# A two-layer decoder trunk: key products on GpSimd, a third weight tile, y turned tile by tile, state copies in sixteen parts

## The reference

```python
def trunk_layer(x, start_pos, conv_buf, pool_buf, k_buf, v_buf, ...):
    h = rms_norm(x, norm_g)
    proj = jnp.einsum('btd,de->bte', h, w_in)
    a_val, a_glu, a_gate, b_val, b_gate, q, k, v, c_gate = jnp.split(proj, cuts, axis=-1)
    u = a_val * jax.nn.sigmoid(a_glu)
    u_ext = jnp.concatenate([conv_buf, u], axis=1)
    c = layer_norm(causal_dwconv(u_ext, conv_w, conv_b), ln_g, ln_b)
    ya = jax.nn.silu(c) * jax.nn.silu(a_gate)
    new_conv = u_ext[:, -(CONV_W - 1):]
    pb_ext = jnp.concatenate([pool_buf, b_val], axis=1)
    yb = multiscale_pool(pb_ext, start_pos, pool_w, pool_scale) * jax.nn.silu(b_gate)
    new_pool = pb_ext[:, -POOL_BUF:]
    q = rope(rms_norm(q, qn_g), pos); k = rope(rms_norm(k, kn_g), pos)
    kk = jnp.concatenate([k_buf, k], axis=1); vv = jnp.concatenate([v_buf, v], axis=1)
    o = dilated_attention(q, kk, vv, k_buf.shape[1])     # 3 patterns: (128,1),(512,4),(2048,16)
    yc = o.reshape(B, T, C_ATT) * jax.nn.silu(c_gate)
    y = jnp.einsum('bte,ed->btd', jnp.concatenate([ya, yb, yc], axis=-1), w_out)
    return x + y, new_conv, new_pool, kk[:, -n_keep:], vv[:, -n_keep:]
```

## Time and profile before

| | us |
|---|---|
| three runs | 416.89, 414.5, 413.16 |
| median | 414.5 |
| the profiled execution, its time | 414.18 |
| its span, first to last instruction | 412.4 |

### The profile page before, as it was taken

One profiled execution on the slowest core, in us unless ns is written; L12 is line 12 of the kernel. 1 busy time (PEld: TensorE's weight loads), 2 busy tenths in 40 slices (PEclk: granted clock), 3 DMA queues, 4 the chain that ended last, 5 costly groups with the idle time before them and its releaser, 6 DMA issues.

```text
span 412.4 us, 4549 instructions
## 1 busy us (share of the span) xinstructions
PE 353.1 (86%) x1552; PEld 272.6 (66%) x1552; DVE 232.0 (56%) x522; ACT 103.3 (25%) x243; POOL 46.3 (11%) x87
## 2 busy tenths in 40 slices
PE   1489799994779969989998999998488968989993
PEld 1368688883457755558876888887366754558872
DVE  1334769859984786331113589979986786331010
ACT  3120013532152422310112011533143422311013
POOL 2410011111101101110010001111111011210000
PEclk9999989999797997999999999999969999999998
DMA  8999999999999999999999999999999999999984
GB/s 282 415 419 417 419 414 360 393 408 378 407 405 417 413 389 385 387 351 418 419 401 412 412 408 381 398 415 351 376 403 418 414 374 370 383 348 333 325 326 186
DMA packets 48836, 158.06 MB, mean 383 GB/s; under 512 B 4644, under 2 KB 18670, under 8 KB 47998
## 3 DMA queue, kind: packets, MB, share of 16 engines
q0 software_dynamic: 21824, 95.11, 60.4%
q1 hardware_dynamic: 17812, 39.36, 25.3%
q10 hardware_dynamic: 9178, 23.31, 14.5%
HBM read 149.39 MB, written 104.42 MB: 615 GB/s over the span
## 4 chain that ended last, share of the span: by engine, by line
PE 46%; DVE 18%; SPq 16%; DMA 14%; issue 2%; ACT 2%; ACTq 0%; DVEq 0%
PE pj L571 17%; PE pj L710 14%; SPq L378 10%; DMA kv<-in_cache_v_win 7%; PE psc L642 7%; DMA kv<-in_cache_k_win 6%; SPq L436 5%; DVE kv L1088 4%; DVE ssc L1091 4%; DVE yc L1148 3%; PE ptr L497 2%; PE ps L519 2%; DVE sc L1058 1%; PE ps L687 1%; PE ps L693 1%
## 5 line engine op out<-in xcount | busy, mean ns | idle before, releaser
L571 PE MATMUL pj<-hT,w 128*128 128x264 f32 x800 | 193.6, 401 | 8.6 <-DVE hT L1010 5.8
L571 PEld LDWEIGHTS pj<-hT,w 128*128 128x128 f32 x800 | 156.1, 198 | 40.2 <-issue 10.3
L1148 DVE SCALAR_TENSOR_TENSOR yc<-u_ext,par,yc 128x256 f32<-128x256 f32 x180 | 76.2, 481 | 2.8 <-DVE u_smp L1038 0.6
L710 PE MATMUL pj<-mix,w 128*128 128x264 f32 x256 | 59.3, 386 | 0.0
L710 PEld LDWEIGHTS pj<-mix,w 128*128 128x128 f32 x256 | 48.5, 190 | 8.2
L485 POOL DMA_DIRECT2D out<-in_cache_v_win x48 | 25.8, 542 | 172.1 <-issue 172.1
L1218 DVE TENSOR_TENSOR xT<-xT,pj 128x264 f32<-128x264 f32 x16 | 6.9, 429 | 53.6 <-PE pj L710 53.6
L485 POOL DMA_DIRECT2D out<-in_cache_k_win x32 | 18.7, 587 | 138.5 <-issue 130.7
L831 ACT ACTIVATE ex<-pj 128x264 f32<-128x264 f32 x22 | 8.6, 391 | 82.6 <-PE pj L571 66.1
L642 PE MATMUL psc<-kv,spm 128*48 128x384 f32 x80 | 27.8, 500 | 1.4 <-DMA kv<-in_cache_v_win 1.4
L937 ACT ACTIVATE hT<-xT 128x264 f32<-128x264 f32 x16 | 6.8, 423 | 66.1 <-DVE xT L1218 66.1
(11 more groups left out here) (169 smaller groups left out, 330.3 us busy)
## 6 DMA issues: line engine op xcount, KB each, us to landing
out<-in_cache_k_win POOLq DMA_DIRECT2D x32, 1512.0 KB, 71.8
out<-in_cache_v_win POOLq DMA_DIRECT2D x16, 1152.0 KB, 72.0
out<-in_cache_v_win POOLq DMA_DIRECT2D x17, 1080.0 KB, 71.1
w<-in_w_out ACTq DMA_DIRECT2D x2, 4096.0 KB, 28.7
out<-in_cache_v_win POOLq DMA_DIRECT2D x16, 432.0 KB, 72.2
w<-in_w_in ACTq DMA_DIRECT2D x1, 4608.0 KB, 31.0
kv<-in_cache_k_win SPq DMA_DIRECT2D x32, 144.0 KB, 24.5
w<-in_w_in ACTq DMA_DIRECT2D x3, 1536.0 KB, 27.6
```

Of the source, the lines that this page charges most:

```text
L571: last = nc.tensor.matmul(pj[n % RING][:, 0:T], wbuf[buf][:, k, col:col + P], hT[:, k, :], start=(k == 0), stop=(k == KD - 1))
L710: last = nc.tensor.matmul(pj[n % RING][:, 0:T], w1[:, k, m * P:(m + 1) * P], mix[:, k, :], start=(k == 0), stop=(k == KD - 1))
L1148: last = V.scalar_tensor_tensor(out=yc[:, t, 0:SEQ], in0=x_w, scalar=par[:, ROW_CW + w * CT + t:ROW_CW + w * CT + t + 1], in1=yc[:, t, 0:S ...
```

## The change

- VectorE's ten products move to GpSimd (`product`), in its queue ahead of copies 20 to 24 (layer 0) and 54 to 58 (layer 1). The first of a layer waits for the gathered keys and for `qb`. VectorE's `sscore` keeps the sums; the five steps stand one projection later in the list, the fifth behind `vtok` 1.
- A third tile `w2` takes b_val and b_gate. So `w0` columns 0 to 767 are free after layer 0's a_glu, and layer 1's a_val and a_glu are loaded behind layer 0's value gather, a_gate once c_gate (now in a_gate's columns) is used.
- In the last layer each tile of `xT` is turned by PE as soon as it is added (`turn_y`), in place of its sum of squares and ACT's Square; ACT, and for one of the four pieces VectorE, copies halves of 4 tiles, and SyncE stores y in five parts.
- The state copies are cut into 16 by 8 pieces in place of 8 rows.
- `so` (output of the sample attention) shares the memory of `rep`, and `spT` turns 48 rows in place of 128; its memset goes.

The diff, cut to what the text speaks of:

```diff
@@ -81,9 +81,9 @@
 PROJ += [("q", t, "w1", t * P) for t in range(AT)]
 PROJ += [("k", t, "w1", C_ATT + t * P) for t in range(AT)]
 PROJ += [("v", t, "w1", 2 * C_ATT + t * P) for t in range(AT)]
-PROJ += [("c_gate", t, "w0", 2 * C_POOL + t * P) for t in range(AT)]
-PROJ += [("b_val", t, "w0", t * P) for t in range(PT_)]
-PROJ += [("b_gate", t, "w0", C_POOL + t * P) for t in range(PT_)]
+PROJ += [("c_gate", t, "w0", 2 * C_CONV + t * P) for t in range(AT)]
+PROJ += [("b_val", t, "w2", t * P) for t in range(PT_)]
+PROJ += [("b_gate", t, "w2", C_POOL + t * P) for t in range(PT_)]
 NPROJ = len(PROJ)
 PIDX = {(g, t): n for n, (g, t, _, _) in enumerate(PROJ)}
 GATES = [(g, t) for g, t, _, _ in PROJ if g in ("a_glu", "a_gate", "c_gate", "b_gate")]
@@ -103,11 +103,11 @@
 SV_CUTS = [(0, 8), (8, 16), (16, SLOTS + 1)]
 _behind = {
     5: ["st0"], 6: ["st1"], 8: ["sconv"],
-    10: [("norm", 0), "conv_p"], 11: [("norm", 1), "conv_s"], 12: [("norm", 2), "rep_q"], 13: [("norm", 3), "qb", ("sscore", 0)],
-    14: [("norm", 4), ("sscore", 1)], 15: [("norm", 5), ("sscore", 2)],
-    16: [("score", 0), "rep_k", ("sscore", 3), ("pnorm", 0)],
-    17: [("probT", 0), ("score", 1), "kb", ("sscore", 4), ("pnorm", 1), "rep_v"],
-    18: [("probT", 1), ("score", 2), ("vtok", 0), ("vtok", 1), ("pnorm", 2), "snew", ("out", 0)],
+    10: [("norm", 0), "conv_p"], 11: [("norm", 1), "conv_s"], 12: [("norm", 2), "rep_q"], 13: [("norm", 3), "qb"],
+    14: [("norm", 4), ("sscore", 0)], 15: [("norm", 5), ("sscore", 1)],
+    16: [("score", 0), "rep_k", ("sscore", 2), ("pnorm", 0)],
+    17: [("probT", 0), ("score", 1), "kb", ("sscore", 3), ("pnorm", 1), "rep_v"],
+    18: [("probT", 1), ("score", 2), ("vtok", 0), ("vtok", 1), ("sscore", 4), ("pnorm", 2), "snew", ("out", 0)],
     19: [("probT", 2), ("score", 3), ("out", 1), "vb", ("pnorm", 3), "ssoft0"],
     20: [("probT", 3), ("score", 4), ("out", 2), ("ktok", 0), ("pnorm", 4), "ssoft1"],
     21: [("probT", 4), ("score", 5), ("out", 3), ("ktok", 1), ("pnorm", 5)],
@@ -176,6 +176,7 @@
 COPIES = [("k", s, a, a + HALF_ROWS) for s in range(NS) for a in (0, HALF_ROWS)]
 COPIES += [("v", s, a, b) for s in range(NS) for a, b in ((0, 768), (768, EVEN_ROWS), (FAR_LO, GATHER[0][0]))]
 IN_FLIGHT = 16
+PRODUCT_AHEAD_OF = {20 + i: (0, i) for i in range(len(SCORE_CUTS))} | {54 + i: (1, i) for i in range(len(SCORE_CUTS))}
 assert DEPTH * len(COPIES) % IN_FLIGHT == 0
 XROUNDS = 5
 
...
@@ -422,10 +425,7 @@
             sp.dma_start(cst[:, early:], const[:, early:]).then_inc(const_in, 16)
 
             for l in range(DEPTH):
-                if l > 0:
-                    sp.wait_ge(S["pj_full"], nth(l - 1, "pj_full", NPROJ))
-                    weights(l, w0, 0, "w_in", COL["a_val"], 3 * C_CONV, "a_in")
-                else:
+                if l == 0:
                     weights(l, w0, 2 * C_CONV, "w_in", COL["a_gate"], C_CONV, "a_gate_in")
 
                 sp.wait_ge(zeroed, 1)
@@ -442,39 +442,62 @@
                     for name in ("v_near_out", "v_far_out"):
                         sp.wait_ge(S[name], nth(l - 1, name, per[name]))
                 gather("k", l, "k_in")
-                sp.wait_ge(S["pj_full"], nth(l, "pj_full", PIDX[("a_gate", CT - 1)] + 1))
-                weights(l, w0, 0, "w_in", COL["b_val"], 2 * C_POOL, "b_in")
+                if l > 0:
+                    sp.wait_ge(S["pj_full"], nth(l - 1, "pj_full", NPROJ))
+                weights(l, w2, 0, "w_in", COL["b_val"], 2 * C_POOL, "b_in")
                 gather("v", l, "v_in", "ks_used")
+                if l < DEPTH - 1:
+                    sp.wait_ge(S["pj_full"], nth(l, "pj_full", PIDX[("a_glu", CT - 1)] + 1))
+                    weights(l + 1, w0, 0, "w_in", COL["a_val"], 2 * C_CONV, "a_val_in")
                 for name, out, keep in (("state_conv", o_conv_s, TAIL - 1), ("state_pool", o_pool_s, POOL_BUF - 1)):
-                    sp.dma_start(out[bass.ds(l, 1), :, 0:keep].rearrange("o s w c -> (o s) (w c)"),
-                                 one(name, l)[:, :, 1:keep + 1].rearrange("o s w c -> (o s) (w c)"))\
+                    sp.dma_start(out[bass.ds(l, 1), :, 0:keep].rearrange("o s w c -> (o s) (w c)").rearrange("s (e x) -> e s x", e=16),
+                                 one(name, l)[:, :, 1:keep + 1].rearrange("o s w c -> (o s) (w c)").rearrange("s (e x) -> e s x", e=16))\
                         .then_inc(S["state_out"], 16)
                 if l < DEPTH - 1:
+                    sp.wait_ge(S["pj_full"], nth(l, "pj_full", PIDX[("c_gate", AT - 1)] + 1))
+                    weights(l + 1, w0, 2 * C_CONV, "w_in", COL["a_gate"], C_CONV, "a_gate_in")
                     params(l + 1)
                     states(l + 1)
                 sp.wait_ge(S["v_in"], nth(l, "v_in", per["v_in"]))
                 put_back_values(l)
-            for r in range(2):
-                sp.wait_ge(y_copied, 2 * r + 2)
-                sp.dma_start(y_prompt.rearrange("b (r p) d -> r p (b d)", p=P)[r], x_tok[:, r * D_MODEL:(r + 1) * D_MODEL]).then_inc(y_out, 16)
-            sp.wait_ge(y_copied, XROUNDS)
+            y_rows = y_prompt.rearrange("b (r p) d -> r p (b d)", p=P)
+            sp.wait_ge(y_copied, 1)
+            sp.dma_start(y_rows[0][:, 0:512], x_tok[:, 0:512]).then_inc(y_out, 16)
+            sp.wait_ge(y_copied, 2)
+            sp.dma_start(y_rows[1][:, 0:512], x_tok[:, D_MODEL:D_MODEL + 512]).then_inc(y_out, 16)
+            sp.wait_ge(y_copied, 4)
+            sp.dma_start(y_rows[0][:, 512:], x_tok[:, 512:D_MODEL]).then_inc(y_out, 16)
+            sp.wait_ge(y_half_copied, 1)
+            sp.dma_start(y_rows[1][:, 512:], x_tok[:, D_MODEL + 512:2 * D_MODEL]).then_inc(y_out, 16)
+            sp.wait_ge(y_copied, 5)
             sp.dma_start(y_sample.rearrange("s t d -> (s t) d"), x_tok[0:NS, 2 * D_MODEL:3 * D_MODEL]).then_inc(y_out, 16)
             sp.wait_ge(bulk_out, 16 * 3)
             for i in range(IN_FLIGHT):
                 sp.wait_ge(copy_out[i], 16 * DEPTH * len(COPIES) // IN_FLIGHT)
             for name in ("v_near_out", "v_far_out", "v_out", "k_out", "new_out", "tail_out", "state_out"):
                 sp.wait_ge(S[name], DEPTH * per[name])
-            sp.wait_ge(y_out, 48)
+            sp.wait_ge(y_out, 80)
 
         @block.gpsimd
         def _(pool):
             for name in START:
                 pool.sem_inc(S[name], 1)
 
+            def product(l, i):
+
+                a, b = SCORE_CUTS[i]
+                if i == 0:
+                    pool.wait_ge(S["k_in"], nth(l, "k_in", per["k_in"]))
+                    pool.wait_ge(S["tr_free"], nth(l, "tr_free", TR["qb"] + 1))
+                nc.gpsimd.tensor_tensor(kv[:, a:b, :], kv[:, a:b, :], qb[:, None, :].to_broadcast([P, b - a, C_ATT]),
+                                        ALU.mult).then_inc(S["kprod_ok"], 1)
+
             pool.wait_ge(x_in, 32)
             for l in reversed(range(DEPTH)):
                 for i, (kind, s, a, b) in enumerate(COPIES):
                     n = (DEPTH - 1 - l) * len(COPIES) + i
+                    if n in PRODUCT_AHEAD_OF:
+                        product(*PRODUCT_AHEAD_OF[n])
                     cache, out = (ins["cache_k_win"], o_k_s) if kind == "k" else (ins["cache_v_win"], o_v_s)
                     if a < FAR_LO or kind == "k":
                         dst = out[l, s, a:b].rearrange("(c e r) h d -> c e (r h d)", c=16, r=PIECE_ROWS)
@@ -513,6 +536,18 @@
                         col = 2 * D_MODEL + k * P
                         last = turn(out[:, k * NS:(k + 1) * NS], x_tok[0:NS, col:col + P], NS)
                 last.then_inc(x_turned, 1)
+
+            def turn_y(k):
+
+                pe.wait_ge(S["xT_ok"], nth(DEPTH - 1, "xT_ok", k + 1))
+                half, c = k // 4, slice(k % 4 * P, k % 4 * P + P)
+                turn(y_banks[half][0][:, c], xT[:, k, 0:P], P)
+                turn(y_banks[half][1][:, c], xT[:, k, P:SEQ], P)
+                if k == 4:
+                    pe.wait_ge(y_copied, 3)
+                last = turn(ptr[0:NS, c], xT[:, k, SEQ:T], P)
+                if k % 4 == 3:
+                    last.then_inc(y_turned, 1)
 
             def sum_squares(k):
 
...
@@ -712,30 +745,18 @@
                         last.then_inc(S["pj_full"], 1)
                         if m == 1:
                             pe.wait_ge(S["st_free"], nth(l, "st_free", NST))
-                        if m >= 1:
-                            pe.wait_ge(S["xsq"], nth(l, "xsq", m))
-                            sum_squares(m - 1)
-                        if m == KD - 1:
-                            pe.wait_ge(S["xsq"], nth(l, "xsq", KD))
-                            sum_squares(m).then_inc(S["st_full"], 1)
-
-
-            pe.wait_ge(S["xT_ok"], nth(DEPTH - 1, "xT_ok", KD))
-            for u in range(XROUNDS):
-                if u >= 2:
-                    pe.wait_ge(y_copied, u - 1)
-                out = (psc, po)[u % 2]
-                r, k0 = u // 2, 4 * (u % 2)
-                if u < 4:
```

(46 more changed lines are left out.)

23 lines of the change are left out of this document (12 added, 11 removed).

## The result

| | before | after |
|---|---|---|
| median of the runs, us | 415.69 (4 runs, 413.16 to 417.0) | 434.52 (4 runs, 433.46 to 438.46) |
| ratio, 95% interval | | 1.0475 (1.0423 to 1.0527) |
| span of the profiled execution | 412.4 | 433.6 |
| mean granted TensorE clock | 0.958 | 0.922 |

What follows compares the result with a forecast made beforehand. The DMA engines with the most work were taken as the bound. Chain 412.4 - 6 - 5 - 3.8 = 397.6, DMA 412.4 - 2.4 = 410.0; the later, plus 1.8 around the span, gave 411.8 us, range 406.5 to 419.

Steps and rivals of the forecast that it cites:

- the terms -6 and -5: Arithmetic chain: moving products to GpSimd lets value gathers leave sooner, -6 us in layer 0, -5 in layer 1.
- rival 1: GpSimd reading SBUF stops VectorE's operations with two SBUF operands: 0 to +8.7 us a layer, at worst 427.8; chance 0.20.
- sums hide beneath: In rival 1's price: VectorE's one-operand sums run under GpSimd's products, 5 x 1.75 = 8.8 us at best.
- P: Time of one GpSimd product of 128x1536: 3.5 us taken, bounds 1.76 and 5.3.
- An issue reads no operands: In rival 1: GpSimd only issued copies there before, so the trace could neither show nor deny the lock.
- price 0: SyncE's queue: early layer 1 weights delay the key gather to near 195, in by about 230, 45 us before use.
- What GpSimd's wait holds up: Copies behind each layer's first product wait 17 or 23 us plus the product; queued copies cover it, no cost.
- the cover of 71.8 us: GpSimd's queue: a copy takes 71.8 us from issue to landing, so that much queued work bridges its waits.
- The DMA side: DMA engines' end: 412.4 - 2.4 = 410.0 us, later than the arithmetic; share stays at 1.02 until about 400, no dip.
- rival 2: The DMA has more to give: half of 11 us between floor and span could go, 408.7 us; chance 0.18.
- The tail: Last layer, y turned by tiles: last store 2.5 us after the last add instead of 6.3, -3.8 on the chain.
- The -2.4 of the states: State copies in 16 by 8 pieces load DMA engines evenly: -2.4 us on the last engine, bounds -2.4 and +2.4.

Runs made afterwards that it cites:

- e2: The changed kernel, products on GpSimd, with layer 1's first weights issued behind the put-backs of values: ratio 1.0464 to the kernel before.
- e8: The kernel before plus unused GpSimd products on scratch tiles, each waiting for the last, with four copies between them: ratio 1.0797.
- e14: The changed kernel with all five products of a layer ahead of one copy, no copies between and no completion wait: ratio 1.0284 to the kernel before.
- e1: The changed kernel with the ten products back on VectorE and their five steps back in their old places: ratio 0.9959 to the kernel before.
- e3: The changed kernel with products and steps back as in e1 and layer 1's weights behind the put-backs as in e2: ratio 0.998 to the kernel before.
- e12: The kernel before with y turned by tiles as the only edit: ratio 0.9982.
- e4: The kernel before with only the ten products moved to GpSimd and their five steps one projection later: ratio 1.0551.
- e11: e3's kernel with the state copies in 8 rows again: ratio 0.9993 to the kernel before.
- e7: The kernel before plus unused GpSimd copies of 128x1536, one operand read, at the ten product places: ratio 1.006.
- e6: The kernel before plus unused GpSimd memsets of 128x3072, writing only, at the ten product places: ratio 1.0015.
- e13: The changed kernel with each GpSimd product waiting until the one before it is complete: ratio 1.0419 to the kernel before.
- e15: The changed kernel with no copies between a layer's products and each product waiting for the one before to complete: ratio 1.0229 to the kernel before.
- e5: The kernel before plus unused GpSimd products of scratch tiles at the ten product places, each waiting for the one before: ratio 1.0505.

## Why the prediction was wrong

- **The step that failed is the terms -6 and -5 in the sum of the chain, and behind them rival 1's price.** They said that handing VectorE's 8.8 us a layer to another engine is worth 6 and 5 us. Measured, the chain is 11.05 and 16.7 us longer, and ends behind the DMA in place of 12 us ahead of it. The mechanism that did it was named, with its rule, and given 0.20, at no more than +8.7 us a layer.
- **In the price the term that was mis-sized is "sums hide beneath".** P came out in number (3.5 taken, 3.43 measured; the products end at 109.7, 109.9 predicted), but its working, VectorE's product and sum added, says nothing of GpSimd: that part is luck. The net of 0 to +8.7 a layer let VectorE do its five sums while products run. But sums stand in VectorE's queue in order, behind taps and norms with two operands. One blocked tap holds back all: in the 19.3 us of products and copies, one sum gets done. What before had followed the first sum, taps, norm and second sum, gets done only once the last product has ended at 109.7: hence +10.0 for the norm and +14.75 for the second sum.
- **What follows was left out.** The price stopped at VectorE. The value gather leaves 14.8 us later, and PE waits 6.4 us for its values in layer 0 (`spv` at 167.35 for 157.73); PE idles 16.9 and 17.2 us, its clock is granted at 0.50 in 100 to 110 and at 0.57 in 300 to 310, and in the ten us behind each it is 0.65 and 0.50. How much of the 21.2 us is the clock's was not separated. In layer 1 the keys come 5.6 us after `qb` on top, and e2, which brings them in time, wins nothing by it.
- **"An issue reads no operands" was right and not enough.** Copies alone do not block, copies between two products do (e8, and the changed kernel against e14).
- **SyncE's queue was mis-sized, without harm.** I counted the weights as 22 us of transfer, so the key gather came out at 195; it started at 246.6. Left out was the time for which SyncE stands in an issue behind weights: 19.2 us for the copy of `state_conv`, where e2, with the weights behind it, takes 3.03. The step "price 0" held, but by luck and not by its cover: of the 45 us to spare none was left. The late keys cost nothing since the lock in the changed kernel (e2) and the DMA in e1 (against e3) cover them.
- **What GpSimd's wait holds up was right in its price.** The price of 0 held: it waited 23.7 and 60.3 us where 17 and 23 were predicted, and the DMA share still stayed at 1.02 and 1.01 between 290 and 310. But of the cover of 71.8 us some 8 were left in layer 1 (an estimate: less the wait of 60.3 and the product of 3.4), so the second wait was mis-sized and the margin luck.
- **The DMA side was right in the main.** Its work was nearly done by 408 where 410.0 was forecast, no dip came, and e3 and e12 show that arithmetic that ends sooner than the DMA is not paid. With the products left on VectorE the time stays within 1% of before: e1 gives 0.9959, e3 0.998. Of rival 2, over 1% faster, no run that makes all its copies shows anything.
- **The tail was right**: 2.5 us predicted, 2.53 in the changed kernel and in e12. Alone it won no time that can be told (e12), as the sum has it; where the arithmetic was the end, some 0.8% by the medians (e4 against the changed kernel), inside the noise. The third weight tile was never run alone; e1 and e3, which have it, show nothing for or against it, as predicted. The -2.4 of the states stays open (e11).

## What to carry to other kernels

Before moving elementwise work from VectorE to GpSimd, list what VectorE has to do in the same stretch: every instruction with two operands in SBUF will stand still while GpSimd reads, and everything behind it in the queue with it, so the move can be expected to pay only where VectorE is idle or has sums and operations from PSUM to do; no run here shows a case where it paid. Price a lock as the whole stretch with the in-order queue behind it, and follow it to the next gather and to PE's clock. And ask first who sets the end: here the arithmetic to be gained was worth nothing, and of the arithmetic lost all that passed the DMA's end was paid: the last store came 24.0 us later, the end of the span 21.2.

## What the runs showed of the hardware

- A GpSimd instruction that reads one SBUF operand shuts out VectorE's two-operand instructions as one with two does (e7: copies of 1.46 us, VectorE's product 3.05 us for 1.76); one that writes only does not (e6: memsets of 2.67 us, the product 1.76).
- The lock can outlast the instruction: 14.3 us over four products of 3.43 with a copy issue between each two and no wait; with a completion wait, or with no copies between, one VectorE instruction passes per product, and the longest takes 4.11 and 3.64 us (e13 to e15). With four copies between scratch products, VectorE's instructions take 5.2 to 5.6 us each, though 2.2 of them are only copy issues (e8).
- It works both ways: GpSimd's instruction took 4.32 us for 3.43 behind VectorE's product (e5).
- One-operand sums (1.75 us) and an operation with one operand in PSUM (0.42 us) kept their length beside it. A one-operand scaling SBUF to SBUF did not: `sc<-sc,rl` of 128x128 took 2.65 and 3.56 us in e8, 0.29 elsewhere.
- SyncE stood 19.2 us in the issue of one 348 KB copy cut into small pieces, and 14.2 us in that of a 1.5 KB row, behind 3.1 and 4.7 MB of weights in its queue; in e2, with layer 1's weights issued later, the same two took 3.03 and 1.77 us (but `conv_b`, also 1.5 KB, 8.50).
